# Hybrid RG-LRU / attention / MLP block: up projection with two-part activations in one 512-column matmul, the halves added on GpSimd

## What is computed

```python
D_MODEL = 2048; SEQ = 512; D_FF = 4 * D_MODEL
...
    h = h + mixed @ w_out[l]
    u = rms_norm(h, norm_mlp_g[l])
    h = h + jnp.square(jax.nn.relu(u @ w_mlp_up[l])) @ w_mlp_down[l]
return rms_norm(h, norm_final_g)
```

## Time and profile before

| what | value |
|---|---|
| median of 3 runs | 2646.97 us (2646.63 to 2647.69) |
| the profiled execution: its time, its span | 2647.3 us, 2645.6 us |
| PE busy over the span | 98% |
| granted TensorE clock, mean | 0.994 |
| input, branches, output projection (steps of the profile until the up pass) | about 0 to 1350 us |
| up pass | about 1350 to 2004 us |
| down pass and last norm | about 2004 to 2646 us |

### The profile page before, as it was taken

The page is one execution under the profiler, slowest core; times in us unless marked ns, Lnnn a source line. Parts: engine busy times, 40 slices in busy tenths (PEclk is TensorE's granted clock), DMA queues, the critical chain, the costliest instruction groups (busy, mean ns, idle before and its releaser), DMA issues.

```text
span 2645.6 us, 37289 instructions
## 1 busy us (share of the span) xinstructions
PE 2593.5 (98%) x14068; PEld 2252.3 (85%) x14068; DVE 1659.3 (63%) x1673; ACT 1155.5 (44%) x1437; POOL 441.1 (17%) x321
## 2 busy tenths in 40 slices
PE   7999999999999999999999999999998899999997
PEld 6888878888888888888889999999997788888886
DVE  5436845433333332242377887787787889999996
ACT  4333354412233232232265565556555445455555
POOL 1000010000000000000001223223222434344343
PEclk9999999999999999999999999999999999999999
DMA  4222322222222222233435655665568865445651
GB/s 174 88 86 80 100 95 97 93 92 86 91 80 83 80 96 95 95 111 127 143 112 191 213 193 179 205 210 179 188 210 297 254 238 209 175 180 213 238 207 80
DMA packets 247374, 394.39 MB, mean 149 GB/s; under 512 B 8832, under 2 KB 156880, under 8 KB 238864
## 3 DMA queue, kind: packets, MB, share of 16 engines
q1 hardware_dynamic: 240848, 373.97, 41.1%
q0 software_dynamic: 5520, 14.16, 2.1%
q10 hardware_dynamic: 944, 5.42, 0.5%
HBM read 326.28 MB, written 67.11 MB: 149 GB/s over the span
## 4 chain that ended last, share of the span: by engine, by line
PE 67%; issue 25%; POOL 3%; DVE 2%; DMA 2%; ACT 1%; ACTq 0%; POOLq 0%; DVEq 0%; SPq 0%
PE stream L1564 15%; PE stream L1565 15%; PE stream L1566 15%; PE aux L1872 3%; PE aux L1874 3%; PE aux L1873 3%; PE stream L1872 3%; PE stream L1873 3%; PE stream L1874 3%; POOL hs L575 2%; POOL hs L578 1%; DMA d<-in_w_mlp_down 1%; DVE dlo L1507 1%; PE aux L1750 1%; DVE d L1461 0%
## 5 line engine op out<-in xcount | busy, mean ns | idle before, releaser
L1061 DVE TENSOR_TENSOR wlo<-raw,whi 128x2048 fp32r<-128x2048 f32 (+1 forms) x113 | 258.1, 2284 | 541.9 <-ACT whi L650 541.8
L1564 PE MATMUL stream<-uhi,whi 128*128 128x512 f32 (+1 forms) x1312 | 511.1, 390 | 0.8 <-ACT rx L722 0.8
L1565 PE MATMUL stream<-ulo,whi 128*128 128x512 f32 (+1 forms) x1312 | 507.5, 387 | 0.0
L1566 PE MATMUL stream<-uhi,wlo 128*128 128x512 f32 (+1 forms) x1312 | 507.4, 387 | 0.0
L650 ACT CAST whi<-raw 128x2048 fp32r<-128x2048 f32 (+1 forms) x113 | 215.4, 1906 | 534.6 <-PE stream L1566 533.8
L1564 PEld LDWEIGHTS stream<-uhi,whi 128*128 128x128 f32 (+1 forms) x1312 | 245.4, 187 | 52.5 <-issue 2.6
L1566 PEld LDWEIGHTS stream<-uhi,wlo 128*128 128x128 f32 (+1 forms) x1312 | 245.2, 187 | 50.2
L1565 PEld LDWEIGHTS stream<-ulo,whi 128*128 128x128 f32 (+1 forms) x1312 | 245.3, 187 | 49.6 <-issue 1.0
L612 POOL TENSOR_TENSOR hh<-hh,dn_tmp 128x512 f32<-128x512 f32 x116 | 222.9, 1942 | 346.7 <-ACT dn_tmp L980 346.7
L1835 PE MATMUL stream<-shi,uwhi 128*128 128x256 f32 x896 | 255.0, 285 | 5.5 <-DVE slo L1336 3.1
L1836 PE MATMUL stream<-slo,uwhi 128*128 128x256 f32 x896 | 254.6, 284 | 0.0
(11 more groups left out here) (258 smaller groups left out, 5120.2 us busy)
## 6 DMA issues: line engine op xcount, KB each, us to landing
raw<-in_w_in SPq DMA_DIRECT2D x80, 1024.0 KB, 5.0
d<-in_w_mlp_down SPq DMA_DIRECT2D x64, 1024.0 KB, 8.3
dsum<-sums_d SPq DMA_DIRECT2D x56, 1024.0 KB, 8.3
up_a<-in_w_mlp_up SPq DMA_DIRECT2D x32, 1024.0 KB, 6.0
up_b<-in_w_mlp_up SPq DMA_DIRECT2D x32, 1024.0 KB, 8.6
sums_d<-hhi SPq DMA_DIRECT2D x32, 896.0 KB, 7.2
sums_d<-hlo SPq DMA_DIRECT2D x32, 896.0 KB, 9.0
raw<-in_w_out SPq DMA_DIRECT2D x16, 1024.0 KB, 5.1
```

The costliest lines, as they stand in the source:

```text
L1061: V.tensor_tensor(wlo[slot][:, 0:width], raw[slot][:, 0:width], whi[slot][:, 0:width].bitcast(F32), ALU.subtract).then_inc(s.lo_ready, 1)
L1564: T.matmul(dst, ah, bh, start=first and k == 0, stop=False)
L1565: T.matmul(dst, ah, bl, start=False, stop=False)
L1566: ins = T.matmul(dst, al, bh, start=False, stop=last and k == n - 1)
```

## The change

Each slice of an up step now has two matmuls: `wl*sh` with 256 columns as before, and `wh` times high and low parts side by side, 512 columns into both halves of the bank. `sums_near` and `sums_far` lay the two parts of the activation sums out for that. The result is then left half plus right half, and the two halves have to be added:

- ACT copies 512 columns in place of 256 for each of the five states (`state[...]`).
- POOL adds the halves of `P1`, `Q5` and `U2` (`merge`), and makes the third output and `c21` (`hid_rest`, three adds): six more operations for each pair.
- DVE's `hid_out` has two operations for each of two outputs, four in place of three.
- `hid_lo` moves from the end of step 6 to the next pair's step 0, behind the subtraction of that step's weights.
- `c21`'s ReLU is an operation of its own behind the copy.
- SP sends the low part of a pair first, and ahead of the weight loads; each part has its own semaphore. In the first down steps the last pairs' spills stand earlier, stage 1 of group 0 loads its weights into buffer 0 (free from `dn_lo` 9 and 10 on), and the last pair's squares and casts stand behind the casts of steps 5 and 7.
- In the first pair some squares of the norm and one weight sum change places.

```diff
@@ up_pe
-                dst = up_bank(u, j)[:, 0:HALF]
+                both, left = halves(up_bank(u, j)), up_bank(u, j)[:, 0:HALF]
...
-                    T.matmul(dst, wh, sh, start=opens and q == 0, stop=False, skip_group_check=not opens)
-                    T.matmul(dst, wh, sl, start=False, stop=False, skip_group_check=not opens)
-                    ins = T.matmul(dst, wl, sh, start=False, stop=q == KP - 1, skip_group_check=not opens)
+                    wh, wl, hl, sh = uwhi[k][:, q], uwlo[k][:, q], ssum[q][:, :, j], shi[q][:, j]
+                    if q:
+                        T.matmul(left, wl, sh, start=False, stop=False, skip_group_check=True)
+                    ins = T.matmul(both, wh, hl, start=opens and q == 0, stop=q == KP - 1, skip_group_check=True)
+                    if q == 0:
+                        T.matmul(left, wl, sh, start=False, stop=False, skip_group_check=True)
@@ gpsimd
-        with pool.Fori(0, PAIRS) as i:
-            hid_sums(i)
+        def merge(i, n):
+            k = ("P1", "Q5", "U2").index(n)
+            pool.wait_ge(s.up_snap, 5 * i + k + 1)
+            pool.tensor_tensor(state[n][:, 1], state[n][:, 1], state[n][:, 0], ALU.add).then_inc(s.up_merge, 1)
+
+        def hid_rest(i):
+            pool.wait_ge(s.up_snap, 5 * i + 4)
+            pool.wait_ge(s.up_merge, 3 * i + 2)
+            v = up_out[:, 2, 0:HALF]
+            pool.tensor_tensor(v, state["Q5"][:, 1], state["U3"][:, 1], ALU.subtract).then_inc(s.up_c22, 1)
+            pool.wait_ge(s.up_c22, 2 * i + 1)
+            pool.tensor_tensor(v, v, state["U3"][:, 0], ALU.subtract).then_inc(s.up_c22, 1)
+            pool.wait_ge(s.up_snap, 5 * i + 5)
+            pool.tensor_tensor(c21, c21, state["A"][:, 0], ALU.add).then_inc(s.up_c21, 1)
+
+        merge(0, "P1")
+        merge(0, "Q5")
+        merge(0, "U2")
+        hid_rest(0)
+        with pool.Fori(1, PAIRS) as i:
+            merge(i, "P1")
+            hid_sums(i - 1)
+            merge(i, "Q5")
+            merge(i, "U2")
+            hid_rest(i)
+        hid_sums(PAIRS - 1)
@@ up_act
                 if j == 1 and not first:
-                    act.wait_ge(s.up_c, 3 * i)
-                    nc.scalar.copy(snap["U3"][:], a_old).then_inc(s.up_snap, 1)
+                    act.wait_ge(s.up_merge, 3 * i - 2)
+                    nc.scalar.copy(state["U3"], a_old).then_inc(s.up_snap, 1)
                 if j == 3 and not first:
-                    nc.scalar.activation(c21[:], a_old, ACT.Relu).then_inc(s.up_snap, 1)
+                    nc.scalar.copy(state["A"], a_old).then_inc(s.up_snap, 1)
...
+        def hid_relu(g, u):
             i = 4 * g + u - 1
-            act.wait_ge(s.up_c, 3 * i + 6)
+            act.wait_ge(s.up_c, 2 * i + 4)
+            act.wait_ge(s.up_c22, 2 * i + 2)
             nc.scalar.activation(up_out[:, :, 0:HALF], up_out[:, :, 0:HALF], ACT.Relu).then_inc(s.up_relu, 1)
-            act.wait_ge(s.up_snap, 5 * i + 5)
+            act.wait_ge(s.up_c21, i + 1)
+            nc.scalar.activation(c21, c21, ACT.Relu).then_inc(s.up_relu, 1)
@@ up_dve
-                if j == 6 and not first:
-                    hid_lo(i - 1)
+                if j == 0 and (not isinstance(i, int) or i >= 2):
+                    hid_lo(i - 2)
...
+            x, n, m, op = {0: (0, "P1", 1, ALU.add), 2: (1, "U2", 3, ALU.subtract)}[j]
+            b, v = up_bank(u, 3 + j), up_out[:, x, 0:HALF]
+            dve.wait_ge(s.up_mm, 7 * i + 8 + j)
+            dve.wait_ge(s.up_merge, 3 * i + m)
...
+            V.tensor_tensor(v, b[:, 0:HALF], state[n][:, 1], op).then_inc(s.up_part, 1)
+            dve.wait_ge(s.up_part, 2 * i + x + 1)
+            V.tensor_tensor(v, v, b[:, HALF:S], ALU.add).then_inc(s.up_c, 1)
@@ sync
         sp.wait_ge(s.up_lo, 7 * 30 + 7)
+        spill(GROUPS - 1, 1)
         load11(0, 0)
         load12(0, 0)
-        spill(GROUPS - 1, 1)
...
         load_sums(0, 1)
+        spill(GROUPS - 1, 2)
         sp.wait_ge(s.up_mm, 4 + 7 * PAIRS)
         load22(0, 0)
-        spill(GROUPS - 1, 2)
...
             if first:
-                sp.wait_ge(s.dn_lo, 14 * st + 12)
...
+                sp.wait_ge(s.dn_lo, 9)
+                load11(0, 1)
+                sp.wait_ge(s.dn_lo, 10)
+                load12(0, 1)
+                spill(GROUPS - 1, 3)
+                sp.wait_ge(s.dn_lo, 12)
@@ dn_act
                 if first and m == 3:
-                    hid_act(GROUPS, 0)
+                    hid_relu(GROUPS, 0)
                 if first and m == 5:
-                    hid_hi(PAIRS - 1)
+                    hid_square(GROUPS, 0)
+                if first and m == 7:
+                    hid_hi(GROUPS, 0)
```

More of the change, by code:

```diff
@@ L260, in hybrid_block @@
     sum_at = [(112, 119), (126, 133), (176, 183), (48, 80), (56, 88), (64, 96), (72, 104), (32, 39)]
-    shi = [at(f"shi{k}", a, [P, 7, HALF], F32R) for k, (a, _) in enumerate(sum_at)]
-    slo = [at(f"slo{k}", b, [P, 7, HALF], F32R) for k, (_, b) in enumerate(sum_at)]
+    sums_near = {k: at(f"sums{k}", sum_at[k][0], [P, 2, 7, HALF], F32R) for k in (0, 1, 2, 7)}
+    sums_far = at("sums_far", 48, [P, 2, 4, 8, HALF], F32R)
+    ssum = [sums_near[k][:] if k in sums_near else sums_far[:, :, k - 3, 0:7] for k in range(8)]
+    shi, slo = ([v[:, c] for v in ssum] for c in range(2))
     up_a = [at("up_a0", 0, [P, 8, 256], F32), at("up_a1", 144, [P, 8, 256], F32)]
@@ L347, in up_bank, with halves, dn_buf, dn_landed @@
         return bank[4 * (u % 2) + "ABC".index(AT[j])]
-    def dn_parts(n, hf):
+    def halves(b):
+        return b[:].rearrange("p (c n) -> p c n", c=2)
+    def dn_buf(g, n):
+        return 0 if isinstance(g, int) and g == 0 else 1 - n
+    def dn_landed(g, n):
+        if isinstance(g, int) and g == 0:
+            return 16 * n + 16
+        return 16 * g + 32 * n
+    def dn_parts(g, n, hf):
         c = slice(2 * hf, 2 * hf + 2)
-        b11, b12, b21, b22, e = d11[n][:, c], d12[n][:, c], d21[:, c], d22[:, c], dn_e[hf][:]
+        d = dn_buf(g, n)
+        b11, b12, b21, b22, e = d11[d][:, c], d12[d][:, c], d21[:, c], d22[:, c], dn_e[hf][:]
         return b11, b12, b21, b22, [b11, e, b11, b21, b12, b22, e]
@@ L416, in spill, with spilled @@
             sp.wait_ge(s.hs_lo, 4 * g + u + 1)
-            for c, v in ((0, hhi), (1, hlo)):
+            for c, v, sem in ((1, hlo, s.hs_spl), (0, hhi, s.hs_sph)):
                 sp.dma_start(sums_d[bass.ds(g, 1), :, :, c, u].rearrange("a q p n -> p (a q) n"),
-                             v[:].bitcast(F32)).then_inc(s.hs_sp[u % 2], 16)
+                             v[:].bitcast(F32)).then_inc(sem[u % 2], 16)
+        def spilled(k, n):
+            sp.wait_ge(s.hs_spl[k], 16 * n)
+            sp.wait_ge(s.hs_sph[k], 16 * n)
         for u in range(4):
-            up_load(u, u, True)
             if u == 3:
                 spill(0, 0)
+            up_load(u, u, True)
         with sp.Fori(1, GROUPS) as g:
             for u in range(4):
+                spill(g if u == 3 else g - 1, (u + 1) % 4)
                 up_load(4 * g + u, u, False)
-                spill(g if u == 3 else g - 1, (u + 1) % 4)
         def dn_load(dst, sem, st, half, c):
@@ L468, in _ @@
         load_sums(0, 5)
-        spill(GROUPS - 1, 3)
         load_sums(0, 6)
-        for k in range(2):
-            sp.wait_ge(s.hs_sp[k], 32 * (PAIRS // 2))
-        load11(0, 1)
-        load12(0, 1)
         def dn_loads(g, n, more, first=False):
@@ L887, in _, with up_act @@
                     squares(i - 1)
-        def up_act(g, u, first, hooks=()):
+        def up_act(g, u, first, hooks={}):
             i = 4 * g + u
@@ L894, in up_act @@
             _, _, _, _, parts = up_parts(u)
[L895 to L896 removed]
+            a, c = halves(up_bank(u, 0)), halves(up_bank(u, 1))
+            a_old = halves(up_bank(u + 1, 0))
             for j in range(7):
@@ L991, in dn_act @@
                 if first and m == 1:
-                    act.wait_ge(s.up_c, 3 * PAIRS)
-                    nc.scalar.copy(snap["U3"][:], up_bank(3, 0)[:, 0:HALF]).then_inc(s.up_snap, 1)
+                    act.wait_ge(s.up_merge, 3 * PAIRS - 2)
+                    nc.scalar.copy(state["U3"], halves(up_bank(3, 0))).then_inc(s.up_snap, 1)
                 if first and m == 3:
-                    nc.scalar.activation(c21[:], up_bank(3, 0)[:, 0:HALF], ACT.Relu).then_inc(s.up_snap, 1)
+                    nc.scalar.copy(state["A"], halves(up_bank(3, 0))).then_inc(s.up_snap, 1)
                 if m == 2 and not first:
@@ L1378, in up_dve @@
                     add(0, up_e[:], b11, b12)
-                if j == (2 if first else 1):
+                if j == 1 and not first:
                     dve.wait_ge(s.up_b[u % 2], loaded)
@@ L1510, in dn_dve @@
                     add(0, dn_e[hf][:], b11, b12)
-                if first and m == 5:
+                if first and m == 0:
+                    hid_lo(PAIRS - 2)
+                if first and m == 7:
                     hid_lo(PAIRS - 1)
```

126 lines of the change are left out of this document (74 added, 52 removed).

## The result

| | before | changed |
|---|---|---|
| median | 2646.94 us (2646.63 to 2647.69, 4 runs) | 2675.39 us (2674.42 to 2676.67, 4 runs) |
| ratio, 95% interval | 1 | 1.0105 (1.0093 to 1.0117) |
| span of the profiled execution | 2645.6 us | 2673.8 us |
| PE's last matmul of the up pass | 2003.37 us | 2029.90 us |
| PE's last matmul of all | 2631.97 us | 2658.54 us |

The kernel is slower by 28.5 us. The forecast was 2667, with 2625 to 2685 around it. The last two rows of the table are starts of single matmuls in the timelines of PE, and they split the 28.2 us of the spans: **26.5 us** come up to the end of the up pass, **0.1 us** between there and the last matmul (628.60 before, 628.64 after), and **1.6 us** behind it.

A forecast was written before the change was run, and what follows sets the result against it. PE sets the pace before; after the change the chain through `hhi`, lengthened by POOL meeting DVE at the port, was to bind. 2647 + 32 (up pass) - 12 (border) = 2667 us, range 2625 to 2685.

The forecast's parts named there:

- The chain and its seven meetings: Up pass: seven POOL operations meet DVE's dense run, 3.8 us, so `hhi` starts every 21.3 us.
- 1.3 to 1.8: Sign expected in the up pass's profile: POOL operations mostly last 1.3 to 1.8 us.
- +32: Up pass: 30 periods of 21.3 against 20.2 us, +33, less some 2 for the first pairs.
- The width's price, 19.42 us for PE: Up pass: PE's work in a pair at 0.2269 and 0.1199 us a matmul, 19.42 us.
- 0.54 us for a meeting: Up pass: a 256-column POOL operation that meets a dense DVE costs DVE 0.54 us.
- The border, -12 us: Border to the down pass: 6 us saved at the first wait, 6 at the second; bounds 0 and 18.
- at 20 to 21 us: Border: the step that started 26.0 us after the loop's last `hhi` is expected at 20 to 21 us.
- The first pair: 0 within 1 us: First pair: the reorder swaps work of the same length before PE's same step, 0 within 1 us.
- PE stays the bound: Rival, up pass: POOL's operations fall into DVE's waits, chain under 19.42 us, 2612 us; chance 0.13.
- Half the meetings: Rival, up pass: two or three POOL operations miss DVE's dense run, period 20.0 to 20.8, 2630 to 2654 us; chance 0.20.
- The clock: Rival: a wait in every pair gives PE the low clock level again and again, 2690 to 2727 us; chance 0.09.

The follow-up runs named there:

- experiment 1: Changed kernel with the wide matmul in all seven steps but without the adds of the right halves (left out of the computation): 2626.38 us, ratio 0.9916.
- experiment 4: Changed kernel with three 256-column matmuls in each slice again, wide copies and six more adds kept: 2672.24 us, ratio 1.0091.
- experiment 5: Kernel before with only the change's moves at the border and its orders; matmuls, copies and adds of before: 2641.66 us, ratio 0.9974.
- experiment 2: Changed kernel without two of POOL's adds from pair 1 on (`U3`'s left half, the halves of A): 2645.91 us, ratio 0.9993.

## Why the prediction held, and where not

**The chain and its seven meetings: right.** The schedule worked out had one `hhi` every 21.3 us; it is 21.16. The seven meetings are the ones named (two of `Q5 - U3`, one before and one behind `hlo`, `c21`, `P1`, three of the four sums), DVE is busy 96% of the pass, most of its lengthened operations last 1.75, and PE waits on `uwlo` twice in each pair. POOL's blocked adds were spread wider than "1.3 to 1.8", from 0.99 to 2.41. ACT's copies of 512 columns take 0.58 to 0.59 us where the text had 0.69. The up pass cost 28.4 us by the last `hhi` of the loop (1995.46 to 2023.84), where +32 was forecast, and 26.5 by PE's last matmul.

**The width's price, 19.42 us for PE: mis-sized by 0.16.** It measured 19.58 when nothing else bound (experiment 1), since the alternation isn't free. In the changed kernel this costs nothing, as experiment 4 shows.

**0.54 us for a meeting: right in the rows, but not always in the chain.** Six of the seven operations are longer by 0.53 to 0.55 and the one that `c21` meets by 0.42. Leaving out two of these meetings gave 0.96, the sum of the two; leaving out `P1`'s gave 0.28, since the leg over ACT's squares and the four sums, which that meeting does not delay, was then what `hhi` waited for.

**The border, -12 us: the step that failed.** The text named `d22` as late next and yet took the step "at 20 to 21 us" behind the last `hhi` of the loop. It came at 23.5 (2047.36 less 2023.84), and the second long wait ended 72.2 us behind it against 73.3 before. From PE's last matmul of the up pass the down pass took as long as before. The moves alone are worth 4.4 us (experiment 5). I had taken them apart from the slower pairs, but a chain that lasts longer than PE's work brings the second last pair's spill to the very place where `d22` is loaded, and the swap of the two gave back 4.8 us in the trace, though not by a shorter first wait. So the two terms of the sum were not independent, which the rivals didn't have either.

**The first pair: 0 within 1 us, about right.** With the moves alone (experiment 5) the pass from PE's first matmul to its last is 0.4 us shorter. **The tail: not in the sum, +1.6**, a port meeting of products of 1024 columns that a later `gfin` caused. Why `gfin` landed later is open.

**The sum.** 2647 + 32 - 12 = 2667 was 8 us under the result. Taken at PE's last matmul of the up pass, the up pass was too high by 5.5 (32 for 26.5), the border too low by 12, and 1.6 for the tail are missing: -5.5 + 12.1 + 1.6 = 8.2, which is the miss between the spans. Two errors partly cancel, so the total came nearer than its border term deserved, and that is luck.

**The rivals.** That PE stays the bound needed fewer than four meetings; there were seven. Half the meetings was no better (and its period was misworked: two or three meetings fewer than seven give 20.2 to 19.7 us at 0.54 each, not 20.0 to 20.8; experiment 2, with two fewer, has 20.20): the add of `c21` began in a PSUM operation of DVE (1631.44 in 1631.30 to 1631.72) and cost the next weight sum 0.42 us all the same. The clock did not fall: it is 1.00 in the stretch above, with a wait of 1.2 us in each pair.
